# Long decays of a recurrence computed on ScalarE, and two attention maps joined in one VectorE pass, in a two-layer block on one core

## The chip, the cores and the metric

One core of one Trainium2 chip runs the whole program. The metric is the device time of that core in microseconds, from its first instruction to its last with what the launch adds; a run is one execution.

## The reference

Two model layers follow each other on 1024 tokens of width 1024, in fp32. The first projects its input with a large matrix and runs eight heads of a gated recurrence (four "gla" heads with values of 256, four "hgrn" heads with values of 128) and four heads of attention over a memory; the second has, among others, eight heads of differential attention. The parts that the change touches compute this:

```
# recurrence, per head: S_t = diag(exp(g_t)) S_{t-1} + k_t v_t^T, o_t = S_t^T q_t
bcum = cumsum(log_g) within a chunk           # log_g of gla is log_sigmoid(...) / TAU, TAU = 16
scores[i, j] = sum_d q[i,d] k[j,d] exp(bcum[i,d] - bcum[j,d])   for j <= i
chunk_kv = (k * exp(b_last - bcum))^T v ;  o_inter = (q * exp(bcum)) state
# differential attention, per head and block of 128 queries, causal
pr = softmax(q k^T)  for two maps m = 0, 1
a  = pr[0] - lam * pr[1]
o  = rms_norm(a @ v) * g * (1 - lam_init), times a gate
```

## The kernel before

**Layout.** The work is written out by hand for the five engines; each engine has a function per phase, and semaphores tie them. Every large projection is done as three fp32r products of a high and a low part (`gemm_part`, L415 to L417 and L426 to L428), in tiles of a 128x512 bank. TensorE works through such tiles also beside everything else: between the steps of the recurrence and of the attention stand "parts" (a quarter of a tile each) of projections that are needed later. ScalarE evacuates finished tiles (`evacuate`, L451), and rounds each block of weights to its high part (`split_high`, L394); GpSimd or VectorE subtracts to get the low part (`split_low`, L381). The order of every engine's work is fixed by the code; nothing is planned at run time.

**Phase 1** computes the log gates: VectorE ends a gla head's at L1025, ScalarE's queue stores them to DRAM, and SyncE loads them back for the recurrence (`load_gates`). Units 0 and 1 of the first head are prepared here already.

**Phase 2, the recurrence.** A head has eight chunks of 128 tokens; two chunks are a unit, so there are 4 units a head and 32 in all. The decay between two tokens of a chunk is split by levels: level j halves blocks of `P >> j` tokens and refers both halves to the cumulated log at the last token of the first half. Level 0 therefore has halves of 64. For each unit VectorE makes (`exponents`, in two parts) the cumulated logs rb with a scan (L1290), then for each of seven levels two subtractions of 128x128 elements (L1298, L1299), part 0 levels 0 to 3, part 1 levels 4 to 6 and the distance to the chunk's end in slot KS of rZ (L1302, 128x256). ScalarE (`decays`) turns each part into exponentials in place with one Exp of 128x1024 (L1316), whose scale is 1/TAU for gla, and makes exp(rb) in slot QS (L1318) and the chunk decays (L1321). GpSimd multiplies levels 0 to 3 with k and q (`operands`), VectorE levels 4 to 6, KS and QS (`short_operands`, L1308). TensorE (`head_pe_rec`) makes the chunk's score products (`rec_products`, L1582 to L1591) and transposes the decayed keys (L1595); VectorE masks (`rec_mask`, L1420), sums (`rec_sum`, L1425) and places them (`rec_place`); TensorE makes the state update (L1539) and the output (L1545, L1547). ScalarE copies the transposed keys (`rec_keys`, L1513), takes the squares of the output (L1476), GpSimd the root, ScalarE normalizes (`normed`, L1506), TensorE turns the result (`rec_turn`, L1568), and VectorE gates it (`gated`, L1442). The bank that `rec_products` of one chunk overwrites holds the turned output of an earlier one, so L1582 waits for `gated`, for the mask, and for the operands of GpSimd and VectorE. `head_dve_rec` works on parts three to five ahead of the chunk at hand. Twelve blocks of weights pass beside the recurrence, so VectorE does twelve low parts between its other work, and ScalarE twelve high parts, ahead of the next `rec_keys` on its queue.

**Phase 6, the differential attention.** For each head and each of its eight query blocks TensorE makes the scores of both maps (L2690), VectorE adds the mask and takes maxima (`scores_max`, L2523 to L2527), ScalarE makes the exponentials with their sums (`attention_exp`, L2623), VectorE inverts both sums (L2471), scales map 1 by -lam over its sum (L2475) and adds map 0 over its sum (L2478); TensorE transposes the joined map (L2656) and multiplies it with v (L2667); ScalarE takes the squares (L2607), GpSimd the root, VectorE normalizes (`outputs_norm`, L2508), TensorE transposes (L2677), VectorE gates (`outputs_gate`, L2513). At a head's end TensorE already makes the next head's first scores, then three parts of a projection, then the last transpose; VectorE ends the head with `outputs_norm` and `outputs_gate` of its last block and begins the next with `scores_max`.

Of the kernel before, what the change touches and what calls it, by code (L numbers as in the profile page):

```python
# [25 lines left out]
ACT = mybir.ActivationFunctionType  # L26
# [50 lines left out]
def build(nc, I, out):  # L77
# [18 lines left out]
    with ctx:  # L96
# [912 lines left out]
        def p1_dve(dve):  # L1009
# [4 lines left out]
            for n in range(2):  # L1014
# [6 lines left out]
                for h in range(2):  # L1021
                    dve.wait_ge(g_act, 4 * n + h + 3)
                    if n:
                        dve.wait_ge(g_st, 32)
                    nc.vector.scalar_tensor_tensor(lg[h][:], lz[:, h, :], 0.0, le[h][:], ALU.min,  # L1025
                                                   ALU.subtract).then_inc(g_dve, 1)
# [50 lines left out]
        class Mixer:  # L1077


            def __init__(self, nv, scale, q, k, at):  # L1080
                self.nv, self.scale, self.q, self.k, self.at = nv, scale, q, k, at

        gla = Mixer(2, 1.0 / TAU, feat1[Q1:, :], feat1[K1:, :], 0)
        hgrn = Mixer(1, 1.0, feat1[HQ - HEADS * P:, :], hgk, HEADS * P)
# [193 lines left out]

        def ahead(head, mixer, after, n):
# [5 lines left out]
        def exponents(dve, head, mixer, u, part):  # L1285
            here = unit_tokens(u)
            if part == 0:
# [4 lines left out]
                dve.wait_ge(r_o, head * 8 + (2 * u + 2))  # L1292
            for j in part_levels(part):
                s = P >> (j + 1)
# [5 lines left out]
            if part == 1:  # L1300
                b3 = rb[:, here].rearrange("p (c n) -> p c n", n=P)
                last = nc.vector.tensor_tensor(rZ[:, u, KS, :].rearrange("p (c n) -> p c n", n=P),  # L1302
                                               b3[:, :, P - 1:P].broadcast_to([P, 2, P]), b3, ALU.subtract)
# [8 lines left out]
        def decays(act, head, mixer, u, part):  # L1312
            here = unit_tokens(u)
            act.wait_ge(r_D, head * 8 + (2 * u + part + 1))
            z = rZ[:, u, 0:FIRST, :] if part == 0 else rZ[:, u, FIRST:KS + 1, :]
            nc.scalar.activation(z, z, ACT.Exp, scale=mixer.scale).then_inc(r_E, 1)  # L1316
            if part == 0:
                nc.scalar.activation(rZ[:, u, QS, :], rb[:, here], ACT.Exp, scale=mixer.scale).then_inc(r_E, 1)  # L1318
                ends = rb[:, here].rearrange("p (c n) -> p c n", n=P)[:, :, P - 1]
                act.wait_ge(r_S, head * 7 + min(2 * u + 2, 7))  # L1320
                nc.scalar.activation(rdec[:, 2 * u:2 * u + 2], ends, ACT.Exp, scale=mixer.scale).then_inc(r_E, 1)  # L1321
# [1143 lines left out]

        def head_dve(dve, it, last_head):
            scores_max(dve, it, 0)
            for qb in range(NT):
                n = (qb + 1) * P
                dve.wait_ge(d_e, it * 16 + (2 * qb + 4))  # L2470
                nc.vector.reciprocal(small[:, 8:10], small[:, 4:6]).then_inc(d_x, 1)  # L2471
                dve.wait_ge(d_x, it * 56 + (7 * qb + 5))
                nc.vector.tensor_tensor(small[:, 10:11], small[:, 9:10], dlam[:, 5:6], ALU.mult).then_inc(d_x, 1)
# [894 lines left out]
```

## Time and profile before

| what | value |
|---|---|
| median of three runs | 2377.93 us (2376.96 to 2381.91) |
| the profiled execution's own time | 2373.18 us |
| its span | 2371.4 us |
| TensorE matmuls busy | 2319.1 us, 98% |
| VectorE busy | 1327.6 us, 56% |
| ScalarE busy | 919.4 us, 39% |
| GpSimd busy | 792.7 us, 33% |
| mean granted TensorE clock | 0.996 |

Times are microseconds, from the start of the span. PE is TensorE, DVE is VectorE, ACT is ScalarE, POOL is GpSimd, SP is SyncE. A line of code is that of the operation or of its helper. A wait is the idle time of an engine before an instruction, with the engine and line that ended it; "issue" is idle time for which the profile shows no releaser. Ends of matmuls are modelled, since they are pipelined; their starts are recorded. The recurrence lies from 325 to 770 us, the differential attention from 1340 to 2055 us.

### The profile page before, as it was taken

What the parts mean: (1) busy time and instruction counts of PE and PEld (TensorE: products, weight loads), DVE (VectorE), ACT (ScalarE), POOL (GpSimd) and SP (SyncE); (2) the same over time, 40 slices, a digit from 0 to 9 for tenths busy, and PEclk for the clock granted to TensorE, in tenths of its full rate; (3) what the DMA queues carried; (4) which work ended last, traced back from release to release, by engine and by line L of the source; (5) the groups of instructions that cost most, each with busy time, mean ns of one, the idle gap of its engine ahead of it and who ended that gap; (6) DMA issues with size and microseconds to landing.
All of it is one profiled execution on the core that took longest, in us unless ns stands there. A gap on an engine that the chain in (4) does not pass through costs nothing.

```text
span 2371.4 us, 37844 instructions
## 1 busy us (share of the span) xinstructions
PE 2319.1 (98%) x14904; PEld 2016.5 (85%) x14904; DVE 1327.6 (56%) x2667; ACT 919.4 (39%) x1698; POOL 792.7 (33%) x707
## 2 busy tenths in 40 slices
PE   8999989999999999999999999999999999999998
PEld 7889978898888899887888898888899888888898
DVE  4003269999997433371333556456456455478746
ACT  5124654444444333332222343343333334465320
POOL 3121334446663221323442333233233242232112
PEclk9999999999999999999999999999999999999999
DMA  6234334443334421232334424314324315375621
GB/s 259 86 128 159 139 133 144 132 143 115 118 130 157 187 98 63 89 124 93 107 108 147 156 71 149 120 67 152 120 68 152 116 72 183 136 277 177 228 92 72
DMA packets 137002, 312.18 MB, mean 132 GB/s; under 512 B 12288, under 2 KB 51840, under 8 KB 125568
## 3 DMA queue, kind: packets, MB, share of 16 engines
q1 hardware_dynamic: 80192, 223.85, 27.6%
q10 hardware_dynamic: 56640, 86.00, 9.9%
q8 instruction: 114, 1.87, 0.3%
q14 instruction: 56, 0.46, 0.1%
HBM read 211.77 MB, written 98.04 MB: 131 GB/s over the span
## 4 chain that ended last, share of the span: by engine, by line
PE 86%; DVE 9%; DMA 2%; issue 1%; ACT 1%; POOL 0%; ACTq 0%; DVEq 0%; SPq 0%; POOLq 0%
PE bank L415 12%; PE bank L417 11%; PE bank L416 11%; PE bank L426 6%; PE bank L427 6%; PE bank L428 6%; PE bank L2690 3%; PE bank L2667 3%; PE bank L2008 3%; PE bank L2010 3%; PE bank L2009 3%; PE bank L507 2%; PE bank L509 2%; PE bank L508 2%; PE bank L2656 1%
## 5 line engine op out<-in xcount | busy, mean ns | idle before, releaser
L415 PE MATMUL bank<-at_hi,w_hi 128*128 128x512 f32 x1408 | 574.2, 408 | 2.4 <-DVE stage L2201 0.9
L417 PE MATMUL bank<-at_hi,w_lo 128*128 128x512 f32 x1408 | 551.2, 391 | 0.0
L416 PE MATMUL bank<-at_lo,w_hi 128*128 128x512 f32 x1408 | 549.7, 390 | 0.0
L381 POOL TENSOR_TENSOR w_lo<-w_raw,w_hi 128x2048 fp32r<-128x2048 f32 x62 | 286.0, 4613 | 495.7 <-ACT w_hi L394 471.7
L426 PE MATMUL bank<-w_hi,at_hi 128*128 128x256 f32 x1280 | 374.5, 293 | 0.5 <-issue 0.5
L428 PE MATMUL bank<-w_hi,at_lo 128*128 128x256 f32 x1280 | 362.8, 283 | 0.0
L427 PE MATMUL bank<-w_lo,at_hi 128*128 128x256 f32 x1280 | 362.8, 283 | 0.0
L415 PEld LDWEIGHTS bank<-at_hi,w_hi 128*128 128x128 f32 x1408 | 265.7, 189 | 61.1 <-issue 8.2
L304 POOL TENSOR_TENSOR small<-small,cols 128x1 f32<-128x1 f32 (+1 forms) x162 | 55.0, 340 | 778.0 <-ACT da_junk L2607 431.6
L417 PEld LDWEIGHTS bank<-at_hi,w_lo 128*128 128x128 f32 x1408 | 264.5, 188 | 57.9
L416 PEld LDWEIGHTS bank<-at_lo,w_hi 128*128 128x128 f32 x1408 | 265.5, 189 | 48.5
L451 ACT ACTIVATE stage<-bank 128x512 f32<-128x512 f32 x216 | 128.6, 595 | 360.5 <-PE bank L417 283.3
L426 PEld LDWEIGHTS bank<-w_hi,at_hi 128*128 128x128 f32 x1280 | 246.2, 192 | 6.8 <-issue 5.2
L427 PEld LDWEIGHTS bank<-w_lo,at_hi 128*128 128x128 f32 x1280 | 246.3, 192 | 0.6
L428 PEld LDWEIGHTS bank<-w_hi,at_lo 128*128 128x128 f32 x1280 | 245.9, 192 | 0.0
L394 ACT ACTIVATE w_hi<-w_raw 128x2048 fp32r<-128x2048 f32 x64 | 122.6, 1915 | 78.1 <-PE bank L428 44.9
L306 POOL TENSOR_TENSOR small<-small,cols 128x1 f32<-128x1 f32 (+1 forms) x162 | 140.1, 865 | 12.7
L2590 ACT ACTIVATE da_aT<-bank 128x512 f32<-128x512 f32 (+2 forms) x96 | 47.2, 492 | 193.9 <-PE bank L2656 186.9
L2513 DVE SCALAR_TENSOR_TENSOR da_y<-bank,da_lam,da_gate 128x128 f32<-128x128 f32 x64 | 22.3, 348 | 176.8 <-PE bank L2677 176.8
L2525 DVE TENSOR_REDUCE small<-bank 128x1 f32<-128x256 f32 (+7 forms) x128 | 97.0, 758 | 4.4
L1346 POOL TENSOR_TENSOR rec_z<-rec_z,rec_k 128x128 f32<-128x128 f32 x128 | 89.8, 702 | 24.8 <-ACT rec_z L1316 24.4
L2623 ACT ACTIVATE da_p<-bank,small 128x256 f32<-128x256 f32 (+7 forms) x128 | 93.4, 739 | 0.2 <-DVE small L2527 0.2
(339 smaller groups left out, 4422.8 us busy)
## 6 DMA issues: line engine op xcount, KB each, us to landing
w_raw<-in_weights SPq DMA_DIRECT2D x84, 1024.0 KB, 7.1
feat<-stage ACTq DMA_DIRECT2D x184, 256.0 KB, 2.0
tok<-stage ACTq DMA_DIRECT2D x72, 256.0 KB, 2.2
stage<-feat SPq DMA_DIRECT2D x32, 256.0 KB, 3.6
w_mem<-in_w_mem SPq DMA_DIRECT2D x4, 1024.0 KB, 7.4
x<-in_x SPq DMA_DIRECT2D x4, 1024.0 KB, 11.3
logg<-gate_g ACTq DMA_DIRECT2D x8, 512.0 KB, 3.0
rec_b<-logg SPq DMA_DIRECT2D x16, 256.0 KB, 4.8
```

Of the source, the lines that this page charges most:

```text
L306: pool.tensor_tensor(to, to, cols[:, ROOT:ROOT + 1].broadcast_to(shape), ALU.pow).then_inc(sem_, 1)
L381: pool.tensor_tensor(w_lo[b][:], w_raw[:, b, :, :], w_hi[b][:].bitcast(F32), ALU.subtract).then_inc(w_split, 1)
L394: nc.scalar.activation(w_hi[b][:], w_raw[:, b, :, :], ACT.Copy).then_inc(w_high, 1)
L415: nc.tensor.matmul(ps_gemm[i % 2], wh, ah, start=(k == 0), stop=False)
L416: nc.tensor.matmul(ps_gemm[i % 2], wh, al, start=False, stop=False)
L417: last = nc.tensor.matmul(ps_gemm[i % 2], wl, ah, start=False, stop=(k == KT - 1))
L426: nc.tensor.matmul(o, ah, wh, start=(k == 0), stop=False)
L427: nc.tensor.matmul(o, ah, wl, start=False, stop=False)
L428: last = nc.tensor.matmul(o, al, wh, start=False, stop=(k == KT - 1))
L451: nc.scalar.activation(stage[:, i, :], ps_gemm[i % 2], s.func, scale=s.scale).then_inc(tile_out, 1)
L2525: nc.vector.reduce_max(small[:, m:m + 1], flat, AX.X).then_inc(d_x, 1)
L2623: nc.scalar.activation(dp[:, m, 0:n], scored(ps, qb), ACT.Exp, bias=small[:, 2 + m:3 + m], scale=DSCALE, accum_out=small[:, 4 + m:5 + m]). ...
```

## The change

In the recurrence level 0 and the KS slot are no longer subtracted by VectorE: ScalarE reads rb itself and takes the reference token as the bias column of its Exp, two pieces of 64 columns a chunk for level 0 and one of 128 for KS. For the second half of level 0 the bias is minus the middle, which VectorE writes with one small product a unit. The factor 1/TAU moves from the Exp to the logs, where phase 1 multiplies by it before they are stored.

In the attention, map 1 is multiplied with -lam l0/l1 and map 0 added in one pass, so the joined map is l0 times what it was; 1/l0 comes in as a second factor of the normalization and as the scale of the squares. The pass over map 1 alone goes. The two inverses lie in columns that alternate by block. The next head's first maxima and exponentials move ahead of the last normalization of a head on VectorE and behind its last squares on ScalarE.

```diff
--- before.py
+++ after.py
@@ -1022,8 +1022,8 @@
                     dve.wait_ge(g_act, 4 * n + h + 3)
                     if n:
                         dve.wait_ge(g_st, 32)
-                    nc.vector.scalar_tensor_tensor(lg[h][:], lz[:, h, :], 0.0, le[h][:], ALU.min,
-                                                   ALU.subtract).then_inc(g_dve, 1)
+                    link(dve, nc.vector.scalar_tensor_tensor(lg[h][:], lz[:, h, :], 0.0, le[h][:], ALU.min, ALU.subtract))
+                    nc.vector.tensor_scalar(lg[h][:], lg[h][:], 1.0 / TAU, None, ALU.mult).then_inc(g_dve, 1)
             first_dve(dve)
             dve.wait_ge(gl_ld, 48)
             with dve.Fori(0, HEADS) as it:
@@ -1077,11 +1077,11 @@
         class Mixer:
 
 
-            def __init__(self, nv, scale, q, k, at):
-                self.nv, self.scale, self.q, self.k, self.at = nv, scale, q, k, at
-
-        gla = Mixer(2, 1.0 / TAU, feat1[Q1:, :], feat1[K1:, :], 0)
-        hgrn = Mixer(1, 1.0, feat1[HQ - HEADS * P:, :], hgk, HEADS * P)
+            def __init__(self, nv, q, k, at):
+                self.nv, self.q, self.k, self.at = nv, q, k, at
+
+        gla = Mixer(2, feat1[Q1:, :], feat1[K1:, :], 0)
+        hgrn = Mixer(1, feat1[HQ - HEADS * P:, :], hgk, HEADS * P)
 
         r_banks = (ps_b[:, 1, :], ps_6)
         ps_keys, ps_kv = ps_7[:, 0:P], ps_b[:, 0, 0:2 * P]
@@ -1276,6 +1276,10 @@
         def part_levels(part):
             return range(FIRST) if part == 0 else range(FIRST, LEVELS)
 
+        def less_middle(u, c):
+
+            return small[:, 16 + 2 * u + c:17 + 2 * u + c]
+
         def ahead(head, mixer, after, n):
 
             return (head, mixer, n // 2, n % 2) if n < 2 * UNITS else (head + 1, after, n // 2 - UNITS, n % 2)
@@ -1290,17 +1294,17 @@
                 nc.vector.tensor_tensor_scan(rb[:, here], reset[:], rb[:, here], 0.0, ALU.mult, ALU.add).then_inc(r_b, 1)
                 dve.wait_ge(r_b, head * 4 + (u + 1))
                 dve.wait_ge(r_o, head * 8 + (2 * u + 2))
+                mids = rb[:, here].rearrange("p (c n) -> p c n", n=P)[:, :, BLK - 1]
+                nc.vector.tensor_scalar(small[:, 16 + 2 * u:18 + 2 * u], mids, -1.0, None, ALU.mult)
             for j in part_levels(part):
+                if j == 0:
+                    continue
                 s = P >> (j + 1)
                 d1, d2 = block_halves(rZ[:, u, j, :], s)
                 b1, b2 = block_halves(rb[:, here], s)
                 mid = b1[:, :, s - 1:s].broadcast_to([P, UNIT // (2 * s), s])
                 nc.vector.tensor_tensor(d1, mid, b1, ALU.subtract)
                 last = nc.vector.tensor_tensor(d2, b2, mid, ALU.subtract)
-            if part == 1:
-                b3 = rb[:, here].rearrange("p (c n) -> p c n", n=P)
-                last = nc.vector.tensor_tensor(rZ[:, u, KS, :].rearrange("p (c n) -> p c n", n=P),
-                                               b3[:, :, P - 1:P].broadcast_to([P, 2, P]), b3, ALU.subtract)
             last.then_inc(r_D, 1)
             if part == 1:
                 dve.wait_ge(r_in_qk[u // 2], head * 32 + 32)
@@ -1312,13 +1316,21 @@
         def decays(act, head, mixer, u, part):
             here = unit_tokens(u)
             act.wait_ge(r_D, head * 8 + (2 * u + part + 1))
-            z = rZ[:, u, 0:FIRST, :] if part == 0 else rZ[:, u, FIRST:KS + 1, :]
-            nc.scalar.activation(z, z, ACT.Exp, scale=mixer.scale).then_inc(r_E, 1)
+            for c in range(2):
+                b = rb[:, u * UNIT + c * P:u * UNIT + (c + 1) * P]
+                if part == 0:
+                    long = rZ[:, u, 0, c * P:(c + 1) * P]
+                    nc.scalar.activation(long[:, 0:BLK], b[:, 0:BLK], ACT.Exp, scale=-1.0, bias=b[:, BLK - 1:BLK])
+                    nc.scalar.activation(long[:, BLK:P], b[:, BLK:P], ACT.Exp, bias=less_middle(u, c))
+                else:
+                    nc.scalar.activation(rZ[:, u, KS, c * P:(c + 1) * P], b, ACT.Exp, scale=-1.0, bias=b[:, P - 1:P])
+            z = rZ[:, u, 1:FIRST, :] if part == 0 else rZ[:, u, FIRST:LEVELS, :]
+            nc.scalar.activation(z, z, ACT.Exp).then_inc(r_E, 1)
             if part == 0:
-                nc.scalar.activation(rZ[:, u, QS, :], rb[:, here], ACT.Exp, scale=mixer.scale).then_inc(r_E, 1)
+                nc.scalar.activation(rZ[:, u, QS, :], rb[:, here], ACT.Exp).then_inc(r_E, 1)
                 ends = rb[:, here].rearrange("p (c n) -> p c n", n=P)[:, :, P - 1]
                 act.wait_ge(r_S, head * 7 + min(2 * u + 2, 7))
-                nc.scalar.activation(rdec[:, 2 * u:2 * u + 2], ends, ACT.Exp, scale=mixer.scale).then_inc(r_E, 1)
+                nc.scalar.activation(rdec[:, 2 * u:2 * u + 2], ends, ACT.Exp).then_inc(r_E, 1)
 
 
 
@@ -2463,19 +2475,29 @@
             for head in range(B_HEADS):
                 head_dve(dve, head, head == B_HEADS - 1)
 
+        def sums_inverse(qb, m):
+
+            return small[:, 16 + 2 * (qb % 2) + m:17 + 2 * (qb % 2) + m]
+
+        def square_scale(qb):
+
+            return small[:, 20 + qb % 2:21 + qb % 2]
+
         def head_dve(dve, it, last_head):
-            scores_max(dve, it, 0)
+            if it == 0:
+                scores_max(dve, it, 0)
             for qb in range(NT):
                 n = (qb + 1) * P
                 dve.wait_ge(d_e, it * 16 + (2 * qb + 4))
-                nc.vector.reciprocal(small[:, 8:10], small[:, 4:6]).then_inc(d_x, 1)
+                both = small[:, 16 + 2 * (qb % 2):18 + 2 * (qb % 2)]
+                nc.vector.reciprocal(both, small[:, 4:6]).then_inc(d_x, 1)
                 dve.wait_ge(d_x, it * 56 + (7 * qb + 5))
-                nc.vector.tensor_tensor(small[:, 10:11], small[:, 9:10], dlam[:, 5:6], ALU.mult).then_inc(d_x, 1)
+                nc.vector.tensor_scalar(small[:, 10:11], sums_inverse(qb, 1), dlam[:, 5:6], small[:, 4:5],
+                                        ALU.mult, ALU.mult).then_inc(d_x, 1)
+                nc.vector.tensor_scalar(square_scale(qb), sums_inverse(qb, 0), P ** -0.5, None, ALU.mult).then_inc(d_x, 1)
                 dve.wait_ge(d_x, it * 56 + (7 * qb + 6))
-                nc.vector.tensor_scalar(dp[:, 1, 0:n], dp[:, 1, 0:n], small[:, 10:11], None, ALU.mult).then_inc(d_x, 1)
-                dve.wait_ge(d_x, it * 56 + (7 * qb + 7))
                 dve.wait_ge(d_at, it * AT_GROUPS + (sum((q + 4) // 4 for q in range(qb)) + 1))
-                nc.vector.scalar_tensor_tensor(da[:, 0:n], dp[:, 0, 0:n], small[:, 8:9], dp[:, 1, 0:n], ALU.mult,
+                nc.vector.scalar_tensor_tensor(da[:, 0:n], dp[:, 1, 0:n], small[:, 10:11], dp[:, 0, 0:n], ALU.mult,
                                                ALU.add).then_inc(d_a, 1)
                 if qb:
                     outputs_norm(dve, it, qb - 1)
@@ -2496,6 +2518,8 @@
                     outputs_gate(dve, it, qb - 1)
             if last_head:
                 outputs_low(dve, 0, range(4))
+            else:
+                scores_max(dve, it + 1, 0)
             outputs_norm(dve, it, NT - 1)
             outputs_gate(dve, it, NT - 1)
             if last_head:
@@ -2505,7 +2529,8 @@
         def outputs_norm(dve, it, qb):
             dve.wait_ge(d_rs, it * 16 + (2 * qb + 2))
             dve.wait_ge(d_F, it * 8 + (qb + 1))
-            nc.vector.tensor_scalar(don[:, qb % 2, :], ps_7[:, 0:P], small[:, 13:14], None, ALU.mult).then_inc(d_on, 1)
+            nc.vector.tensor_scalar(don[:, qb % 2, :], ps_7[:, 0:P], small[:, 13:14], sums_inverse(qb, 0),
+                                    ALU.mult, ALU.mult).then_inc(d_on, 1)
 
         def outputs_gate(dve, it, qb):
             dve.wait_ge(d_F, it * 8 + (qb + 3))
@@ -2575,7 +2600,8 @@
             eng.dma_start(dg[head % 2][:], feat2[ZB + row:ZB + row + P, :]).then_inc(d_in_g, 16)
 
         def head_act(act, it):
-            attention_exp(act, it, 0)
+            if it == 0:
+                attention_exp(act, it, 0)
             slot_results(act, it, FIRST_SLOT)
             g = 0
             for qb in range(NT):
@@ -2604,9 +2630,10 @@
                 if it == B_HEADS - 1 and qb == NT - 1:
                     outputs_high(act, 0, range(4))
                 act.wait_ge(d_o, it * 8 + (qb + 2))
-                nc.scalar.activation(djunk[:], ps_7[:, 0:P], ACT.Square, scale=P ** -0.5,
+                nc.scalar.activation(djunk[:], ps_7[:, 0:P], ACT.Square, scale=square_scale(qb),
                                      accum_out=small[:, 12:13]).then_inc(d_ss, 1)
             if it < B_HEADS - 1:
+                attention_exp(act, it + 1, 0)
                 slot_results(act, it, LAST_SLOT)
             else:
                 outputs_high(act, 0, range(4, 7))
```

## Rows read from the trace of the kernel before

**Rows 1.** Busy us (x instructions) of each engine by stretch, then PEclk, DMA, GB/s
```profile
325.00:356.00 31.00, 24.66 (x230) 19.73 (x228) 27.95 (x73) 16.02 (x29) 14.38 (x22) 1.00 0.43 149
356.10:359.40 3.30, 3.30 (x14) 2.72 (x11) 3.27 (x13) 0.64 (x2) 0.00 (x0) 0.50 0.33 119
356.00:727.00 371.00, 362.41 (x3200) 313.81 (x3198) 358.71 (x1019) 165.35 (x381) 205.31 (x324) 1.00 0.40 131
1345.00:2050.00 705.00, 704.98 (x4472) 606.95 (x4472) 384.95 (x815) 277.08 (x617) 228.44 (x174) 1.00 0.34 116
```

**Rows 2.** Waits of PE, 356 to 770 us: us in total, times, longest us
```profile
PE bank L1582 <- DVE rec_mx L1442: 7.1, 9, 1.2
PE bank L1539 <- issue: 1.4, 1, 1.4
```

**Rows 3.** Waits of PE, 325 to 360 us
```profile
PE bank L1582 <- DVE rec_mx L1442: 2.7, 1, 2.7
PE bank L1568 <- DVE fill L1420: 1.7, 1, 1.7
PE bank L1582 <- issue: 1.6, 2, 1.3
```

**Rows 4.** Timeline of PE around one pause: start us, us, instruction, idle before
```profile
582.94 0.40 PE L417 MATMUL bank<-at_hi,w_lo 128*128 128x512 f32 x1
584.14 0.41 PE L1582 MATMUL bank<-rec_z 128*128 128x64 f32 x2 [0.81 <-DVE rec_mx L1442]
```

**Rows 5.** Timeline of DVE: subtractions, one beside GpSimd, a head's first maxima
```profile
508.49 0.28 DVE L1299 TENSOR_TENSOR rec_z<-rec_b 128x128 f32<-128x128 f32 x1
508.69 0.42 DVE L1302 TENSOR_TENSOR rec_z<-rec_b 128x256 f32<-128x256 f32 x1
509.03 0.42 DVE L1308 TENSOR_TENSOR rec_z<-rec_z,rec_q 128x256 f32<-128x256 f32 x1
...
578.49 0.55 DVE L1347 TENSOR_TENSOR rec_z<-rec_z,rec_q 128x128 f32<-128x128 f32 x1
...
1428.55 0.29 DVE L2523 TENSOR_TENSOR bank<-bank,causal 128x128 f32<-128x128 f32 x1
...
1429.20 0.15 DVE L2527 TENSOR_SCALAR small<-small 128x1 f32<-128x1 f32 x1
1429.27 0.29 DVE L2523 TENSOR_TENSOR bank<-bank,causal 128x128 f32<-128x128 f32 x1
```

**Rows 6.** Groups of ACT, 325 to 770 us: busy us, mean ns, idle
```profile
L1316 ACT ACTIVATE rec_z<-rec_z 128x1024 f32<-128x1024 f32 x60 | 63.1, 1052 | 7.3 <-DVE rec_z L1302 5.3 <-DVE rec_z L1299 2.0
...
L1513 ACT ACTIVATE rec_kT<-bank 128x128 f32<-128x128 f32 x56 | 15.4, 275 | 40.0 <-PE bank L1595 37.4 <-ACT stage L451 1.2 <-DVEq L294 1.1
...
L1318 ACT ACTIVATE rec_z<-rec_b 128x256 f32<-128x256 f32 x30 | 12.1, 403 | 0.0
L1506 ACT ACTIVATE rec_on<-bank,small 128x128 f32<-128x128 f32 x32 | 11.6, 362 | 12.8 <-POOL small L306 12.4 <-ACT stage L451 0.5
```

**Rows 7.** Timeline of ACT and of PE: weight split, key copy, key product
```profile
566.30 1.91 ACT L394 ACTIVATE w_hi<-w_raw 128x2048 fp32r<-128x2048 f32 x1 [0.50 <-ACT stage L451]
568.12 0.26 ACT L1513 ACTIVATE rec_kT<-bank 128x128 f32<-128x128 f32 x1
...
568.48 0.35 PE L1539 MATMUL bank<-rec_v,rec_kT 128*128 128x128 f32 x1 [1.45 <-issue]
```

**Rows 8.** Groups of DVE, 1345 to 2050 us: the pass over one map
```profile
L2475 DVE TENSOR_SCALAR da_p<-da_p,small 128x1024 f32<-128x1024 f32 x8 | 6.0, 753 | 0.3
```

**Rows 9.** Timeline at a head's end: DVE's normalization, PE's transpose of it
```profile
1424.49 0.35 DVE L2508 TENSOR_SCALAR da_on<-bank,small 128x128 f32<-128x128 f32 x1 [1.88 <-POOL small L306]
...
1427.98 0.27 PE L2677 MATMUL bank<-ident,da_on 128*128 128x128 f32 x1
```

**Rows 10.** Timeline of POOL: the level products of one unit
```profile
506.21 3.56 POOL L1346 TENSOR_TENSOR rec_z<-rec_z,rec_k 128x128 f32<-128x128 f32 x1 [0.19 <-ACT rec_z L1316]
509.73 0.47 POOL L1347 TENSOR_TENSOR rec_z<-rec_z,rec_q 128x128 f32<-128x128 f32 x1
```

## The prediction

> **What bounds the kernel now.** I read first the page's busy shares (in the table ahead): TensorE leads the other engines by far. Such an average only says that a change off TensorE can be worth at most TensorE's pauses, so next come stretches [rows 1]. From 1345 to 2050 us, the attention, TensorE is busy for 704.98 of 705 us. From 356 to 727 us, the recurrence, it is busy for 362.41 of 371 us while VectorE is busy for 358.71: two engines near their limit side by side. From 325 to 356 us, the recurrence's first chunks, TensorE is busy for only 24.66 of 31 us. The view of waits then names who ends TensorE's pauses. In the recurrence proper nine of them, 7.1 us together and 1.2 us at most, stand before L1582, the first product of a chunk, and end with VectorE's L1442 (`gated`, which empties the bank that the products overwrite); one of 1.4 us stands before L1539 [rows 2]. In the first chunks there are 2.7, 1.7 and 1.6 us, all before work that VectorE must release: L1582 twice over, and L1568 behind the mask L1420 [rows 3]. A pause costs a little more than the view says, since it counts from a modelled end: at 582.94 the last matmul of the tile beside starts, at 584.14 L1582, 1.20 us where an ordinary step is 0.23, and the view has 0.81 us [rows 4]. So each of the nine costs about 0.97 us against 0.81, and the nine 7.1 + 9 x 0.16 = 8.5 us.
>
> **The recurrence, VectorE.** A unit is two chunks; there are 32, of which 30 fall behind the first 325 us. Per unit the change removes two subtractions of level 0 (L1298, L1299) and the 128x256 subtraction L1302. In a back-to-back run the next operation starts 0.20 us after the small one and 0.34 us after L1302 [rows 5], so 0.20 + 0.20 + 0.34 = 0.74 us go. When GpSimd works beside, the same shape lasts 0.55 us in place of 0.28 (578.49) [rows 5], a step of 0.47 us with the same overlap, and the saving is up to 0.47 + 0.47 + 0.34 = 1.28 us. What comes is one 128x2 product by -1. No row has that shape; the 128x1 L2527 takes a step of 0.07 us (1429.20 to 1429.27) and lasts 0.15 us [rows 5], which bounds it; I take 0.10, since it is two elements. Net 0.64 us per unit, 19 us of VectorE's work over 30 units, against 8.5 us of pauses that it causes. A pause appears when VectorE has fallen behind by a w_lo split (L381); it now regains 0.32 us per chunk more, 1.7 us in the 5.3 chunks between two splits (12 splits in 64 chunks), more than the longest pause of 1.2 us. But pauses that come one or two chunks behind a split have only 0.3 to 0.6 us of help. I take 85%: **-7.2 us** (bounds -4 and -8.5).
>
> **The first chunks.** Between 332 and 354 us VectorE runs without a gap; by the code four of the removed groups lie in it (parts 0 and 1 of units 2 and 3): 0.41 + 0.34 + 0.41 + 0.34 less two small products, 1.3 us. The pauses there total 6.0 us [rows 3]. One of them is also close to ScalarE, so I take **-1.0 us** (0 to -1.5). Behind these pauses the granted clock is 0.50, the lower of the two levels, from 356.1 to 359.4 us [rows 1]; these 3.3 us hold half their work, so 1.7 us would come back if the clock stayed. I leave it in place: the pause of 2.7 us becomes shorter but does not vanish.
>
> **The recurrence, ScalarE.** Part 0 gets four Exp of 128x64 with a bias column in place of 256 columns of the big one, part 1 two of 128x128. From the groups [rows 6]: 1024 columns 1052 ns and 256 columns 403 ns give 0.845 ns a column and 187 ns fixed; 128 columns from a bank cost 275 ns plain (L1513) and 362 ns with a column as scale (L1506), so a pointer is 87 ns. Neighbours overlap by about 0.1 us (the 1.91 us split at 566.30 and the copy at 568.12 [rows 7]). Part 0: 4 x (187 + 54 + 87 - 100) = 0.91 less 0.22 = +0.70 us; part 1: 2 x (187 + 108 + 87 - 100) = 0.56 less 0.22 = +0.35 us. That is 1.05 us per unit, 31 us over 30 units. ScalarE has room for the sum, but not at every place: all that stands behind the decays on its queue comes later, the bank's evacuation, the next tile's w_hi split and then L1513 (`rec_keys`), for which TensorE's L1539 waits. The 1.4 us pause is this one: w_hi at 566.30, L1513 at 568.12, L1539 at 568.48 [rows 7]. A w_hi split can stand ahead of a key copy at most twelve times (12 blocks of weights); at those the delay of 0.35 to 0.7 us meets little slack. I take **+0.8 us** (0 to +4). The 1.4 us pause itself was made by a late normalization, which hung on GpSimd and VectorE; **-0.5 us** (0 to -1.4). The product by 1/TAU in phase 1 adds to VectorE four 128x1024 operations with a constant, each with a wait on the one before: 0.75 us each by L2475's [rows 8], 0.9 with the wait, 3.6 us in all. Behind them hang ScalarE's stores of the logs (at most 2 us later, the evacuations behind them too) and SyncE's loads of the first gates; TensorE's projections hide that, and without them it would cost its 2 us.
>
> **Attention.** Each of the 64 query blocks loses a VectorE pass of up to 0.75 us [rows 8] and gains a 128x1 product; a column takes the place of ScalarE's constant scale, at 87 ns [rows 6]. All are nothing for the end: TensorE pauses for 0.02 us in 705 [rows 1], and no product is moved. The step with a risk is the order at a head's end: VectorE now handles the next head's first scores before `outputs_norm`: three operations a map, one map 0.72 us (1428.55 to 1429.27) [rows 5], so 1.4 us. The normalization L2508 runs at 1424.49 and TensorE's transpose of it starts at 1427.98 [rows 9], 3.1 us behind its end, so 1.4 us are covered; ScalarE's two Exp (0.36 us each by L1506 [rows 6], 0.6 us with the overlap) go before an evacuation that has some 3 us to wait for its tile. No DMA is issued or moved. **0 us** (0 to +1).
>
> **Sum.** -7.2 - 1.0 + 0.8 - 0.5 = -7.9 us. The profiled execution took 2373.18 us (span 2371.4), 4.75 us below the median of the three runs, 2377.93. So 2365.3 against its own time, and about **2370 us** as a median.
>
> **A rule weighed.** GpSimd's first level product at 506.21 lasts 3.56 us, the next 0.47 [rows 10]: it stood still while VectorE ran its two-input operations back to back, and later VectorE was the one that slowed, to 0.47 us a step [rows 5]. The Trainium skill, SBUF — State Buffer, section "SBUF: two separate sides", says that VectorE operations with two SBUF inputs and GpSimd's share a port pair which goes whole to whoever starts first. By that rule fewer two-input operations are a gain, but the small one-input product put in front of the burst is also a gap in which GpSimd can take the pair; the trace shows both orders of it, and by the rule the sum would change sign where GpSimd is waiting each time.
>
> **The rivals.**
> (a) *The wait changes hands.* VectorE's help is real, but ScalarE's later evacuations, splits and key copies make TensorE wait before L1539 or L415. For it: the 1.4 us pause. Against: ScalarE is busy for 165.35 of 371 us [rows 1]. Its bound of +4 with VectorE's -4 to -7.2 leaves -1 to -4: about 2375 us.
> (b) *Slower: GpSimd gets in at the small product.* Then the six steps of levels 1 to 3 take 0.47 instead of 0.20 us: 1.6 us per unit against 0.64 saved. It decides from the point where this happens in 40% of the units (0.64/1.6). In all units VectorE has 30 x 0.96 = 29 us more work; its gaps take up 371 - 358.7 = 12 us of that [rows 1], some 15 us reach TensorE: 2393 us. Against: GpSimd's level products begin when part 0's Exp have ended (506.21) [rows 10], so they lie beside part 1, which gets no small product.
> (c) *More comes back.* All nine pauses, 1.4 us at L1539, 1.5 us at the start and the clock's 1.7: -13 us, 2365 us.
> (d) *Attention pays after all*: excluded as a gain by its 0.02 us of pauses.
>
> **How the numbers follow.** Forecast 0.57; (a) 0.22; (b) 0.05; (c) 0.16. A measurement of this kernel tells about 0.2%, 4.8 us, from no change. Faster by more: most of the forecast's case (its weakest corner, -4, lies outside), all of (c), a little of (a): 0.74. Within: 0.21. Slower: (b), 0.05. The range reaches from (c), with a little for the spread of the runs, to (a)'s weak end: 2363 to 2376.5 us.
>
> **What the profile after would show.** Right: L1442 releases L1582 two times or fewer; VectorE busy about 20 us less from 325 to 770 us; ScalarE about 30 us more there; attention unchanged. Wrong: pauses before L1539 behind ScalarE (a); steps of 0.47 us in L1298's bursts of part 0 (b); any pause before L2677.

## The result and the profile after

The changed kernel takes 2365.51 us (median of 4 runs, 2364.55 to 2368.91), the kernel before 2378.99 us beside it (4 runs, 2376.96 to 2381.91): ratio 0.995, interval 0.9935 to 0.9966, faster by 8 to 15 us. Forecast: 2370.0 us, 7.9 us less. Direction and range held; in the medians the gain is 13.5 us. Its profiled execution took 2368.91 us (span 2367.1), the longest of its four.

The page's busy time, span share and instructions by engine, of after:

```profile
PE 2321.3 (98%) x14904; PEld 2020.3 (85%) x14904; DVE 1244.1 (53%) x2607; ACT 960.9 (41%) x1890; POOL 784.5 (33%) x707
```

Stretches of after, columns as in [rows 1]. It begins the recurrence 2.0 us later (328.06 against 326.06 us), so the second, fourth and last of these lines answer to [rows 1] step for step:

```profile
325.00:356.00 31.00, 25.69 (x211) 20.52 (x209) 26.71 (x68) 20.05 (x42) 12.72 (x22) 1.00 0.42 145
328.00:358.00 30.00, 24.89 (x230) 20.40 (x231) 27.91 (x72) 17.50 (x42) 12.72 (x22) 0.98 0.47 163
356.00:727.00 371.00, 367.15 (x3260) 320.30 (x3260) 326.09 (x981) 195.44 (x546) 211.26 (x324) 0.99 0.39 132
358.00:723.00 365.00, 361.15 (x3196) 315.00 (x3197) 320.15 (x964) 194.18 (x542) 209.84 (x322) 0.99 0.39 133
646.90:650.10 3.20, 3.20 (x9) 2.45 (x8) 3.17 (x12) 0.48 (x2) 0.00 (x0) 0.50 0.00 0
1342.00:2047.00 705.00, 705.00 (x4472) 606.98 (x4471) 338.20 (x816) 283.91 (x614) 216.52 (x174) 1.00 0.34 116
```

TensorE's 3196 matmuls took 371 us before [rows 1, 3200 of them] and take 365 now. In the attention VectorE is 47 us less busy for the same 4472 matmuls in the same 705 us. Who ends TensorE's pauses (us in total, times, longest), from 325 to 356 us and, below the dots, from 356 to 770 us:

```profile
PE bank L1594 <- DVE rec_mx L1454: 2.6, 1, 2.6
PE bank L1594 <- issue: 1.3, 2, 1.0
PE bank L1580 <- DVE fill L1432: 1.0, 1, 1.0
PE bank L1551 <- issue: 0.4, 1, 0.4
...
PE bank L1594 <- DVE rec_mx L1454: 2.5, 2, 1.5
PE bank L1551 <- issue: 1.3, 3, 0.7
PE bank L426 <- issue: 0.3, 1, 0.3
```

L1594, L1454, L1580, L1432 and L1551 are L1582, L1442, L1568, L1420 and L1539 of before. The nine pauses of [rows 2] are two. VectorE is the surprise. Its groups of the two longest bursts and of the small product, 325 to 770 us (busy us, mean ns):

```profile
L1306 DVE TENSOR_TENSOR rec_z<-rec_b 128x128 f32<-128x128 f32 x180 | 52.1, 289 | 0.0
...
L1358 DVE TENSOR_TENSOR rec_z<-rec_z,rec_k 128x128 f32<-128x128 f32 x93 | 27.6, 297 | 0.0
...
L1298 DVE TENSOR_SCALAR small<-rec_b 128x2 f32<-128x2 f32 x30 | 5.3, 176 | 1.0
```

The same groups of a second profile of before (2377.74 us):

```profile
L1298 DVE TENSOR_TENSOR rec_z<-rec_b 128x128 f32<-128x128 f32 x210 | 65.5, 312 | 1.0
...
L1346 DVE TENSOR_TENSOR rec_z<-rec_z,rec_k 128x128 f32<-128x128 f32 x93 | 33.3, 358 | 0.0
```

L1346 is untouched by the change (now L1358), and yet each became 61 ns shorter. It is 0.28 us when alone and 0.55 us when GpSimd works beside it.

**How the traces are counted below.** A *slow step* is a distance of 0.4 to 0.7 us from the start of a VectorE operation on rec_z to the start of VectorE's next operation; otherwise it is 0.20 us behind a 128x128 one and 0.34 us behind a 128x256 one. A *pause* is what a step between TensorE's starts has above its usual length, from 0.25 us. A *dip* is a stretch of some 3.4 us at a granted clock of 0.50, the lower of the two levels; one of 6.8 us counts as two. *Length* goes from the first product of scores to the last turn of the recurrence (L1582 and L1568 before).

### The profile page after: what moved, and what is told of

The parts are those of the page before. It is cut to its first block, busy times and chain, and to the rows that moved or that the text cites. A ratio compares the mean times of both kernels' runs of the same rounds, so it can differ in the third digit from the quotient of the medians.

```text
span 2367.1 us, 37976 instructions
## 1 busy us (share of the span) xinstructions
PE 2321.3 (98%) x14904; PEld 2020.3 (85%) x14904; DVE 1244.1 (53%) x2607; ACT 960.9 (41%) x1890; POOL 784.5 (33%) x707
## 4 chain that ended last, share of the span: by engine, by line
PE 93%; DVE 3%; ACT 1%; DMA 1%; issue 1%; POOL 0%; ACTq 0%; DVEq 0%; POOLq 0%; SPq 0%
PE bank L415 13%; PE bank L417 13%; PE bank L416 13%; PE bank L426 6%; PE bank L427 6%; PE bank L428 6%; PE bank L2717 3%; PE bank L2694 3%; PE bank L2020 3%; PE bank L2021 3%; PE bank L2022 3%; PE bank L1599 2%; PE bank L507 2%; PE bank L509 2%; PE bank L508 2%; PE bank L2683 1%
## 5 line engine op out<-in xcount | busy, mean ns | idle before, releaser
L1358 POOL TENSOR_TENSOR rec_z<-rec_z,rec_k 128x128 f32<-128x128 f32 x128 | 95.1, 743 | 38.3 <-ACT rec_z L1328 38.3
```

Of the source, the lines that this page charges most:

```text
L1358: eng.tensor_tensor(z1, z1, k1, ALU.mult)
```

## The experiments

The medians of the kernel before stand beside each kernel's own and are of the same chip. What each kernel is stands in the sections below.

| kernel | median us, before's | ratio (interval) | length us | pauses us | slow steps |
|---|---|---|---|---|---|
| before, two profiles | | | 444.6, 448.7 | 18.2, 20.5 | 94, 93 |
| att_only | 2378.52, 2379.30 | 0.9998 (0.9988 to 1.0009) | 445.2 | 19.0 | 75 |
| after, two profiles | 2365.51, 2378.99 | 0.995 (0.9935 to 0.9966) | 438.5, 435.8 | 11.6, 10.6 | 21, 13 |
| rec_only | 2364.41, 2379.30 | 0.9942 (0.9928 to 0.9956) | 434.2 | 10.4 | 13 |
| dve_back | 2373.90, 2379.85 | 0.9967 (0.9956 to 0.9979) | 445.2 | 18.3 | 37 |
| level0_back | 2374.49, 2379.85 | 0.9977 (0.9968 to 0.9987) | 444.8 | 18.9 | 90 |
| no_split | 2368.10, 2379.85 | 0.9949 (0.9934 to 0.9964) | 435.2 | 9.9 | 76 |
| order_mid | 2381.49, 2379.85 | 1.0000 (0.9991 to 1.0009) | 450.3 | 20.4 | 136 |
| exp_pieces | 2377.13, 2379.57 | 0.9987 (0.9978 to 0.9995) | 448.3 | 19.6 | 36 |
| pieces_tau | 2376.86, 2377.79 | 0.9995 (0.9984 to 1.0005) | 445.6 | not counted | 28 |
| gate_before | 2365.03, 2379.57 | 0.9942 (0.9929 to 0.9955) | 434.8 | 9.1 | 1 |
| gate_after | 2361.18, 2379.57 | 0.9925 (0.9913 to 0.9938) | 431.5 | 7.4 | 2 |

### The halves: rec_only, att_only, and both kernels again

rec_only is before with the diff's hunks up to `decays`, att_only before with those from `sums_inverse` on; after_again and before_again are the two kernels unchanged.

> The recurrence's part alone (long decays by ScalarE, 1/TAU in the logs), attention as before. If the whole gain lies in the recurrence, the time is that of the full change, about 0.4 to 0.5% below before, and the recurrence (first score product to last turn) is 6 us or more shorter than the 444.6 us of before. If attention gave the part that my sum lacks, this stays at about -8 us (-0.3%).

> Attention's part alone (one pass, 1/l0 at the output, next head's first maxima earlier), recurrence as before. My theory: TensorE has no pause there, so the time stays within 0.1% of before and the attention stretch within 0.3 us of 712.9 us. Rival: attention brings the missing 5 us, then -0.2%.

> The changed kernel unaltered, a second profile. If executions repeat, the recurrence takes 438.5 us again within 0.5 us, and TensorE's pauses before its score products stand at the same chunks. If executions differ in how ScalarE, GpSimd and VectorE fall against each other, the length moves by 2 us or more and the pauses stand elsewhere.

> The kernel before unaltered, a second profile. Its first profiled execution took 2373.18 us, below all its other runs (2376.96 to 2381.91). If that one was a lucky execution, this one shows a longer recurrence than 444.6 us, by about 4 to 8 us, and the same lengths elsewhere; else the recurrence repeats at 444.6 us and the difference lies in another stretch.

rec_only has the whole gain, 14.9 us; att_only has none. Its attention, from the stretches of att_only:

```profile
1345.00:2050.00 705.00, 704.40 (x4469) 606.26 (x4469) 337.21 (x816) 284.95 (x616) 216.91 (x174) 1.00 0.34 117
```

after_again: 2366.50 us, ratio 0.9943 (0.9927 to 0.996). Its recurrence is 2.7 us shorter than in after's first profile, so executions do differ: a pause of 1.0 us for `gated` and the second dip are missing. before_again also has nine pauses for `gated`, but only six of them within 1 us of the places of [rows 2]; its waits of TensorE, 356 to 770 us:

```profile
PE bank L1582 <- DVE rec_mx L1442: 7.6, 9, 1.9
PE bank L1539 <- issue: 3.6, 2, 2.2
```

Length less pauses less 1.7 us a dip (one, two and one in before, before_again and att_only; two, one and none in after, after_again and rec_only) is 423.5 to 424.8 us in all six. The mean length falls from 446.2 to 436.2 us; of these 10.0 us, 8.3 are pauses (19.2 to 10.9), 0.6 dips, and about 1 is in neither. The same difference is 423.5 to 424.2 us in the other kernels whose pauses are counted, but 426.5 us in order_mid.

### Is it VectorE's work, or its order? dve_back, level0_back, order_mid

dve_back lets VectorE subtract what ScalarE then overwrites:

```diff
--- after.py
+++ dve_back.py
             for j in part_levels(part):
-                if j == 0:
-                    continue
...
+            if part == 1:
+                b3 = rb[:, here].rearrange("p (c n) -> p c n", n=P)
+                last = nc.vector.tensor_tensor(rZ[:, u, KS, :].rearrange("p (c n) -> p c n", n=P),
+                                               b3[:, :, P - 1:P].broadcast_to([P, 2, P]), b3, ALU.subtract)
```

> The changed kernel with VectorE's three subtractions a unit put back (ScalarE overwrites their results), so VectorE has its old work and the small product, and ScalarE its new work. My theory, that the gain is VectorE's relief: the time returns to before or a little above it, +0 to +4 us, ScalarE's work being worth about +0.8. If ScalarE's pieces by themselves cost much (rival a), it ends +5 us or more above before, with pauses ahead of the key product. If the gain came from the exponents being ready sooner or from the prescaled logs, it stays 5 us or more below before.

6.0 us are gained although no subtraction is saved, where my theory had 0 to +4 us; some 7.5 are lost against after. VectorE's smaller work, with the slow steps that it avoids (37 here, 21 and 13 in after), is about half of the matter. level0_back gives level 0 back whole, with one Exp of 128x1024 for part 0, and leaves KS with ScalarE:

```diff
--- after.py
+++ level0_back.py
-                nc.vector.tensor_scalar(small[:, 16 + 2 * u:18 + 2 * u], mids, -1.0, None, ALU.mult)
             for j in part_levels(part):
-                if j == 0:
-                    continue
...
-                if part == 0:
-                    long = rZ[:, u, 0, c * P:(c + 1) * P]
...
-                else:
+                if part:
...
-            z = rZ[:, u, 1:FIRST, :] if part == 0 else rZ[:, u, FIRST:LEVELS, :]
+            z = rZ[:, u, 0:FIRST, :] if part == 0 else rZ[:, u, FIRST:LEVELS, :]
```

> The changed kernel with level 0 given back to VectorE and to the one Exp, KS alone by ScalarE: VectorE keeps 0.34 of the 0.64 us a unit. If the gain follows VectorE's work in proportion, about half of it is left, -5 to -8 us. If most pauses go with the first relief, nearly all is left, -10 us or more.

VectorE has one operation less a unit and 5.4 us are gained; the slow steps are those of before. Its waits of TensorE, 356 to 770 us:

```profile
PE bank L1586 <- DVE rec_mx L1446: 8.3, 8, 2.4
PE bank L1543 <- issue: 3.4, 3, 1.7
```

So level 0's move carries most, by fewer subtractions or by what ScalarE's longer part 0 does to GpSimd. order_mid moves VectorE's long bursts between the sums and the state update:

```diff
--- after.py
+++ order_mid.py
-                if c % 2 == 0 and (after or c + 3 < 2 * UNITS):
-                    short_operands(dve, *ahead(head, mixer, after, c + 3)[:3])
-                if after or c + 5 < 2 * UNITS:
-                    exponents(dve, *ahead(head, mixer, after, c + 5))
...
                     rec_sum(dve, *then)
+                if c % 2 == 0 and (after or c + 3 < 2 * UNITS):
+                    short_operands(dve, *ahead(head, mixer, after, c + 3)[:3])
+                if after or c + 5 < 2 * UNITS:
+                    exponents(dve, *ahead(head, mixer, after, c + 5))
```

> The changed kernel with VectorE's operands and subtractions moved behind the masked sum and ahead of the state update of the same chunk, so that the bank is emptied sooner. By my theory the pauses that end with the emptied bank go, the recurrence is 424 to 432 us and the time 3 to 8 us below the changed kernel. Rival: the state and the placed scores come later and TensorE waits ahead of the output product, same or slower.

I had expected 3 to 8 us less than after. The gain is gone, with all of the saved work still saved: VectorE's multiplications (levels 4 to 6, KS and QS) now fall on GpSimd's run, 129 of their 247 steps slow. Their group on VectorE, 297 ns each in after:

```profile
L1358 DVE TENSOR_TENSOR rec_z<-rec_z,rec_k 128x128 f32<-128x128 f32 x93 | 42.1, 453 | 0.0
```

The move also puts the state update behind the bursts, and TensorE then waits before L1551 twelve times, 10.0 us; which part is whose this kernel does not tell.

### Who puts VectorE behind: no_split

```diff
--- before.py
+++ no_split.py
-                split_low(dve, n // 2, n % 2)
+                dve.wait_ge(w_high, n + 1)
+                w = n % 2
+                dve.tensor_tensor(w_lo[w][:, 0, 0:8], w_raw[:, w, 0, 0:8], w_hi[w][:, 0, 0:8].bitcast(F32),
+                                  ALU.subtract).then_inc(w_split, 1)
```

> The kernel before with the eleven or twelve low parts of the weights that VectorE makes inside the recurrence cut to eight columns (the low parts of those blocks are left out). If pauses arise when VectorE falls behind by a split, nearly all pauses after the first 40 us go and the recurrence takes 430 to 436 us in place of 445 to 449, with the first 35 us unchanged. If VectorE's steady work is the bound, about 25 us of its work less still leaves pauses.

Waits of TensorE, 356 to 770 us:

```profile
PE bank L1585 <- DVE rec_mx L1445: 2.7, 1, 2.7
PE bank L1542 <- issue: 1.3, 1, 1.3
PE bank L426 <- issue: 0.3, 1, 0.3
```

The one wait left for `gated` is that of the first chunks. The nine are gone with 76 slow steps still there, and in gate_before below with every split still there: in these runs a pause needs both, VectorE behind by a split and too slow to catch up. Without the splits VectorE also has some 23 us less to do, which this kernel does not separate from their place.

### Where VectorE and GpSimd meet: exp_pieces, pieces_tau

All 94 slow steps of before lie inside GpSimd's runs of level products. There are 30 such runs; 15 of them hold slow steps, 13 four or more. GpSimd starts its run when part 0's Exp have ended. To start it later without touching VectorE's work, exp_pieces cuts the Exp:

```diff
--- before.py
+++ exp_pieces.py
-            z = rZ[:, u, 0:FIRST, :] if part == 0 else rZ[:, u, FIRST:KS + 1, :]
-            nc.scalar.activation(z, z, ACT.Exp, scale=mixer.scale).then_inc(r_E, 1)
+            w = P if part == 0 else 2 * P
+            for j in range(4):
+                for at in range(0, UNIT, w):
+                    z = rZ[:, u, j + part * FIRST, at:at + w]
+                    last = nc.scalar.activation(z, z, ACT.Exp, scale=mixer.scale)
+            last.then_inc(r_E, 1)
```

> The kernel before with its one Exp of 128x1024 in eight pieces of 128 columns (part 0) or four of 256 (part 1): the same arithmetic, ScalarE about 0.6 and 0.3 us later with its result, VectorE's work untouched. New theory: a later start keeps GpSimd's level products out of VectorE's run of two-input operations, so it is faster than before by 4 to 8 us and VectorE's steps of 0.4 to 0.7 us fall from about 94 to about 40. Rival: ScalarE's time is only a cost, then 0 to +2 us, and the gain of the kernel with VectorE's work put back came from the prescaled logs.

pieces_tau adds the change's product by 1/TAU on the logs and takes the scale off the Exp.

> The kernel with the Exp in pieces, and with 1/TAU moved into the logs as in the changed kernel: against the kernel with VectorE's work put back, what is left different is that ScalarE takes level 0 and KS from the cumulated logs with a bias column, and the small product. If the prescaled logs made the 3 to 5 us between those two, this one is at -6 to -8 us against before; if they are worth nothing, it stays at -1 to -4 us like the pieces alone.

Slow steps fall from 94 to 36, as expected, and only 2.4 us come, where 4 to 8 were. Waits of TensorE in exp_pieces, 356 to 770 us:

```profile
PE bank L1586 <- DVE rec_mx L1446: 5.8, 4, 1.9
PE bank L1543 <- issue: 4.7, 3, 1.8
```

The meeting changed sides: level products of GpSimd that last over 1 us, held up by VectorE's bursts, rise from 13 (45 us) to 19 (52 us), its roots over 1 us from 13 (39 us) to 19 (53 us), and late roots make late normalizations and key products; that chain is argued from the order of the work. In after the same two counts are 21 (48 us) and 21 (50 us), so there too the meeting changed sides, and what after has beyond exp_pieces is above all VectorE's smaller work. The scale in the logs is worth nothing that shows.

### One wait: gate_before, gate_after

GpSimd's run is kept back until VectorE has finished its subtractions of part 1 of the same unit. The same line is put into both kernels:

```diff
             pool.wait_ge(r_in_qk[u // 2], head * 32 + 32)
+            pool.wait_ge(r_D, head * 8 + (2 * u + 2))
             pool.wait_ge(r_E, head * 16 + (4 * u + 1))
```

> The kernel before, with GpSimd's level products of a unit waiting also until VectorE has made the unit's part 1 subtractions. New theory (the two engines slow each other when their runs meet): VectorE's slow steps fall to below 50 and the time by 4 to 8 us with no operation removed. Rival: only the amount of VectorE's work counts, or the gate holds back the operands and the roots behind them: no gain or a loss.

> The same gate on the changed kernel, which has only about 20 slow steps left. New theory: little to win, 0 to -3 us against the changed kernel. If it is slower than the changed kernel by 2 us or more, the gate's delay of GpSimd's roots costs more than the meeting of the runs.

gate_before removes no instruction and gains 14.5 us, as much as the change and more than the 4 to 8 us expected. Its timeline of GpSimd (start us, us, instruction, idle before):

```profile
503.50 0.55 POOL L306 TENSOR_TENSOR small<-small,cols 128x1 f32<-128x1 f32 x1
507.40 0.53 POOL L1347 TENSOR_TENSOR rec_z<-rec_z,rec_k 128x128 f32<-128x128 f32 x1 [3.36 <-DVE rec_z L1302]
507.90 0.46 POOL L1348 TENSOR_TENSOR rec_z<-rec_z,rec_q 128x128 f32<-128x128 f32 x1
```

GpSimd waits for 3.36 us in place of the product of 3.56 us in [rows 10]: in this unit it loses nothing, and over all units VectorE has one slow step left, and GpSimd 3 level products of over 1 us (7.5 us) in place of 13 (45 us). Waits of TensorE in gate_before, 325 to 770 us:

```profile
PE bank L1540 <- issue: 3.6, 2, 2.1
PE bank L1569 <- DVE fill L1421: 2.0, 1, 2.0
PE bank L1583 <- issue: 1.6, 2, 1.3
PE bank L426 <- issue: 0.3, 1, 0.3
PE bank L1596 <- ACT rec_kT L1514: 0.2, 1, 0.2
```

None for `gated` is left. And in gate_after, with one of 0.8 us left for `gated`:

```profile
PE bank L1552 <- issue: 2.3, 4, 1.2
PE bank L1595 <- issue: 1.3, 2, 1.0
PE bank L1581 <- DVE fill L1433: 1.1, 1, 1.1
PE bank L1595 <- DVE rec_mx L1455: 0.8, 1, 0.8
PE bank L426 <- issue: 0.3, 1, 0.3
```

gate_after at 2361.18 us is the best kernel of the study: 15 to 21 us under before, and in the medians 4 to 5 us under after, where 0 to 3 were expected (from other chips, and the two intervals against before just touch). With the meeting out of the way the change is still worth 3.9 us (2365.03 to 2361.18); without the gate it is worth 13.5. This suggests that most of those 13.5 us come by fewer or cheaper meetings, and about 4 us by the smaller work itself. The runs also lie closer together: 2363.41 to 2366.41 for gate_before (5 runs), 2376.30 to 2382.26 for before on that chip (17 runs).

## Why the prediction was right or wrong

**What bounds.** Right: VectorE's `gated` behind a split is the wait, and no_split, which takes the splits away, takes all nine pauses away.

**Steady recurrence, -7.2 (nine pauses).** The count was right, two left ("two times or fewer"), with 2.5 us of 7.1 (2.9 of 8.5 start to start, so -5.6). Its reason was half of the matter. VectorE's busy time fell by 40 us within the recurrence (418.4 to 378.3), not the 19 of the forecast: the other 20 are 73 slow steps fewer at 0.27 us. I had both prices from [rows 5], 0.20 and 0.47 us, and used the dearer one only for operations that go, never for those that stay beside GpSimd. No run gives that term alone: exp_pieces removes 58 slow steps and gains 2.4 us while GpSimd's long operations grow, and gate_before removes 93 of them together with GpSimd's long level products and gains 14.5 us.

**The longest pause left** is at 643.25 to 645.18 us, 1.53 us, and has slow steps ahead of it. VectorE of after, from the split on:

```profile
636.69 2.28 DVE L381 TENSOR_TENSOR w_lo<-w_raw,w_hi 128x2048 fp32r<-128x2048 f32 x1
...
639.97 0.55 DVE L1358 TENSOR_TENSOR rec_z<-rec_z,rec_k 128x128 f32<-128x128 f32 x1
...
642.43 0.54 DVE L1306 TENSOR_TENSOR rec_z<-rec_b 128x128 f32<-128x128 f32 x1
...
644.70 0.34 DVE L1454 SCALAR_TENSOR_TENSOR rec_mx<-bank,norm_half,rec_gate 128x128 f32<-128x128 f32 x1
```

GpSimd at the same time:

```profile
636.70 2.67 POOL L306 TENSOR_TENSOR small<-small,cols 128x1 f32<-128x1 f32 x1
639.35 0.55 POOL L1358 TENSOR_TENSOR rec_z<-rec_z,rec_k 128x128 f32<-128x128 f32 x1
```

The split holds GpSimd's root of 128x1 for 2.67 us, so its level products start at 639.35, in the middle of VectorE's bursts, and eight steps there are slow.

**First chunks, -1.0.** The view's pauses there went from 6.0 to 5.3 us, -0.7; the long one is 2.6 us as before, where I had it shortened. The dip behind it stayed, as assumed (3.4 us from 356.7). A second dip, 646.9 to 650.1 us, follows the pause of 1.53 us; of the three profiles with the change in the recurrence only this one has it, and it holds 1.6 us.

**ScalarE, +0.8.** 33 us busier within the recurrence (198.5 to 231.3), 31 forecast. Its groups in after:

```profile
L1328 ACT ACTIVATE rec_z<-rec_z 128x768 f32<-128x768 f32 x60 | 49.8, 830 | 0.0
...
L1326 ACT ACTIVATE rec_z<-rec_b 128x128 f32<-128x128 f32 x60 | 20.5, 391 | 3.7 <-DVE rec_z L1307 3.7
L1323 ACT ACTIVATE rec_z<-rec_b 128x64 f32<-128x64 f32 x60 | 20.2, 337 | 0.7 <-DVE rec_z L1307 0.7
L1324 ACT ACTIVATE rec_z<-rec_b,small 128x64 f32<-128x64 f32 x60 | 20.1, 335 | 0.0
```

I had worked out 187 + 54 + 87 = 328 and 187 + 108 + 87 = 382 ns. The Trainium skill, ScalarE: Activation LUTs, section "What ACT_TABLE_LOAD costs", gives 186 ns plus 0.833 ns an element and about 93 ns a pointer operand, 332 and 386; the trace agrees within 5 ns. As for the end, three short pauses before L1551 (1.3 us in all) stand where one of 1.4 us stood, so the +0.8 and the -0.5 for the key product come to 0 together against before's first profile. Rival (a) had no room. What I missed is the other face of this cost: part 0's Exp now take 1.69 in place of 0.95 us, from the first start to that of the instruction behind them, and GpSimd starts that much later.

**Attention 0, 1/TAU 0.** Right (att_only, pieces_tau). At the head's end the maxima stand ahead of the normalization (L2532, L2508 of before) at 1421.40 us, and TensorE's transpose of it (L2704, L2677 of before) starts at 1424.25, 2.4 us behind the normalization's end.

**Rival (b).** The right resource at the wrong place: no step of part 0's bursts is slow in any of the 30 units. The small product costs 0.07 us to the next start (631.38 to 631.45) and lets nobody in. The rule I weighed, the Trainium skill's SBUF — State Buffer, section "SBUF: two separate sides", says that the pair goes, for the whole instruction, to whoever starts first. The trace agrees for GpSimd, held for 2.67 us by one split. But in [rows 10] one GpSimd operation stands still through a whole burst of VectorE's, whose steps stay at 0.20 us ([rows 5], from 508.49 us), and not just one operation; elsewhere both advance in turns. From the timelines of before, VectorE and, below the dots, GpSimd:

```profile
578.01 0.56 DVE L1346 TENSOR_TENSOR rec_z<-rec_z,rec_k 128x128 f32<-128x128 f32 x1
578.49 0.55 DVE L1347 TENSOR_TENSOR rec_z<-rec_z,rec_q 128x128 f32<-128x128 f32 x1
...
577.97 0.46 POOL L1346 TENSOR_TENSOR rec_z<-rec_z,rec_k 128x128 f32<-128x128 f32 x1
578.38 0.51 POOL L1347 TENSOR_TENSOR rec_z<-rec_z,rec_q 128x128 f32<-128x128 f32 x1
578.86 0.51 POOL L1346 TENSOR_TENSOR rec_z<-rec_z,rec_k 128x128 f32<-128x128 f32 x1
```

The turns add 0.27 us to VectorE's step of 0.20 and 0.05 to GpSimd's of 0.42: in turns the slower partner sets the pace. A common step of 0.47 us is also less than 0.20 and 0.42 us together, so the two overlap in part. At 577.14 us GpSimd's run was under way before VectorE's burst; at 639.35 us it came into the burst, and they took turns all the same. When a burst locks GpSimd out instead, as in [rows 10], no run settles.

**The sum, and where its size failed.** In the recurrence the traces give 19.2 - 10.9 = 8.3 us of pauses, beside the forecast's 7.2 + 1.0 + 0.5 = 8.7. That these agree is in part luck: the first two profiles alone give 18.2 - 11.6 = 6.6 us, and the relief of VectorE behind them is twice what I had counted. The step that failed is the last one, "2365.3 against its own time, and about 2370 us as a median": I took the 4.75 us by which that execution lay below the median as a constant that the change leaves alone. Before's second profile has a recurrence 4.1 us longer, all of it pauses and a dip, which is the sort that the change removes. Its three profiles (att_only's with them) took 2373.18 to 2377.74 us, under the median of 2379; the three with the change in the recurrence took 2363.52 to 2368.91 us. The means of the two groups are 8.7 us apart, near the forecast's 7.9, but the medians 12.8 to 14.9 us. That the executions at the median have more such pauses still is argued, not seen. Rival (c)'s time, 2365 us, is the one that came, though not by its terms: two of the nine pauses, the long one of the first chunks and the clock's dip are still there.

**Open.** dve_back and exp_pieces have about as many slow steps (37 and 36), and yet medians 3.2 us apart. In their profiles the lengths differ by 3.1 us: 1.3 us of pauses, and 1.7 us of dips (three of 3.4 us in exp_pieces, one of 6.8 us in dve_back, 1.7 us lost for each 3.4). What makes those differ is open. Both profiles of after start the recurrence 2 us late and that of rec_only does not; gate_before does and gate_after does not, so it goes with neither the change nor the gate, and was not pursued. Why a pause of 1.5 us is followed by a dip in one execution and not in the next is open as well.

## What to carry to other kernels

Before costing VectorE's operations next to GpSimd's, list the distances between their starts: if one shape has two values, ask which steps will meet after the change, since those that stay may bring as much as those that go. A single wait that keeps GpSimd's run out of VectorE's long bursts gave 14.5 us here, as much as the whole change, and the two together gave 18.4. Profile a kernel more than once before taking the gap between a profile and the median as constant.

## What the runs showed of the hardware

- VectorE's 128x128 operation with two SBUF inputs: step 0.20 us alone, 0.47 us in turns with GpSimd's products, whose own step goes from 0.42 to some 0.47 us. That is VectorE at less than half its pace and GpSimd nearly undisturbed.
- The other way round GpSimd stands still: a 128x1 operation lasted 2.67 us beside VectorE's low part, a 128x128 one 3.56 us beside a burst [rows 10]. Which of the two comes when, no run here settles.
- One VectorE operation on 128x2 elements lasts 176 ns in its group and delays the next by 0.07 us.
- The spread of a kernel's executions can come from such meetings: 6 us for before on one chip (17 runs), 3 us with the gate (5 runs, so a hint rather than a measure).
